# Interleaving the projections and the attention ranges of two head groups, token tile by token tile

## The chip, the cores and the metric

The kernel runs on the 8 cores of one Trainium2 chip. Every core runs the same program on one prompt sequence of 2048 tokens and four of the 32 sample tokens, so each core handles 2052 token columns. No data goes from core to core. The time is that of the device, in microseconds, of the slowest core.

## The reference

One step of a hybrid decoder layer:

```
x += 0.5 * SwiGLU(RMSNorm(x))                         # half-step FFN 1
z  = RMSNorm(x) @ w_in                                # one input projection
A: 3 groups x 4 heads x 128, (window, dilation) = (128,1), (512,4), (2048,16)
   query t reads keys t, t-d, ..., t-window; the three outputs of a head slot are
   merged with weights proportional to their softmax denominators
B: HGRN2 recurrence, 4 heads, state 128x128
C: 4-head cross attention into 256 memory tokens
x += (sum of gate_i * branch_i @ w_i) @ w_out
x += 0.5 * SwiGLU(RMSNorm(x)); final RMSNorm
```

D_MODEL is 1024 and D_FF 2816. Besides y, the kernel returns the last keys and values of each group, the memory keys and values, the recurrent states and the shifted caches of the sample tokens.

## The kernel before, in words

The program has three parts: FFN 1 (to about 495 us of the profiled span), the mixer stage with the branches A, B and C (about 495 to 1030 us), and the merge with FFN 2. The change lies in branch A of the middle stage.

**Order of the work.** The kernel is written as a list of operations with read and write dependencies (class `Prog`). A planner orders them for each engine when the program is built. An operation's priority is the TensorE time written ahead of it in its branch; `merge` stretches the three branches ("att" over 0 to 1, "hg" over 0.03 to 0.97, "mem" over 0 to 0.95) over the same stretch of time. On each engine the planner takes the ready operation of lowest priority number. A buffer is given out only to one of the first n waiting requests of its pool, where n is the number of free buffers. On the chip each engine then runs its list in order and waits on semaphores.

**Pools.** `ps`: 8 PSUM banks, which the whole kernel shares. `wp`: 6 buffers for weights (`wload`, issued by GpSimd, with a lead of 45000 ns on the priority). `s4`: 11 buffers of 128x2048 bf16, for q, k, v and P16. `s1`: 18 buffers of 128x512 bf16. `fw`: 8 buffers of 128x512 f32.

**Branch A, head slot s** (`att_head`). Group 2 (dilation 16) comes first: `att_group` loads its weights, projects q and k (`qk_proj`, five token tiles `QT` of 416, 416, 416, 400 and 404 columns, 8 matmuls each), then v (`v_proj`, four ranges of 512 tokens, 32 matmuls with 128 columns each, and the sample columns). Four score banks give P16. Then group 1 (dilation 4) is projected whole, then group 0 (dilation 1) is projected whole, and then `att_range` runs for R = 0, 1, 2, 3 in a row. A range of 512 tokens is 11 to 16 score matmuls into three or four banks, one exp per bank on ScalarE, one mask multiplication per bank on VectorE, four to five additions on VectorE for the denominators, 31 to 32 matmuls into the bank `num`, one matmul with ones into `den`, Ln and Exp for the reciprocal on ScalarE, and one multiplication on VectorE. `att_sample` ends the head.

**Dependencies.** Each of q, k, v has a single dependency record for its 2048 columns: a copy of one tile into it waits for all matmuls written earlier that read any part of it.

**Pacing.** `pace`, called at the end of each range, marks a point after which SyncE may issue one of the cache copies (`spread`, DRAM to DRAM); the copies are assigned to the nearest mark. Most matmuls are recorded at line 703 (`mm`), ScalarE functions at 707 and 709, copies at 714 and 716, `tensor_tensor` at 722, weight loads at 739. Line 1134 clears 128 columns once per head, in range 0.

Of the kernel before, what the change touches and what calls it, by code (L numbers as in the profile page):

```python
# [595 lines left out]
QT = [(0, 416), (416, 416), (832, 416), (1248, 400), (1648, 404)]  # L596
# [3 lines left out]
def build_nc():  # L600
# [3 lines left out]
    def din(name, shape):  # L604
        return nc.dram_tensor(name, list(shape), F32, kind="ExternalInput").ap()
# [13 lines left out]
    w_qkv = din("w_qkv", [12, 128, 3072])  # L619
# [38 lines left out]
    def xrb(byte0, nbytes):  # L658
        return xr[:, byte0 // 4:(byte0 + nbytes) // 4].bitcast(BF16)
    s4 = P.pool("s4", [xrb(i * 4096, 4096) for i in range(8)] + [xrb(HA * 4 + i * 4096, 4096) for i in range(3)])  # L660
# [38 lines left out]
    def hdeps(c, t0, n):  # L699
        return [dh[i][c] for i in range(6) if TOFF[i] < t0 + n and t0 < TOFF[i] + TW[i]]  # L700

    def mm(o, l, r, start, stop, rd, wr):
        P.op(PE, lambda e: e.matmul(o(), lhsT=l(), rhs=r(), start=start, stop=stop, skip_group_check=True), reads=rd, writes=wr)  # L703
# [7 lines left out]
    def evac(o, i, rd, wr, engs=(ACT, DVE)):  # L711
        alts = {}
        if ACT in engs:
            alts[ACT] = lambda e: e.copy(out=o(), in_=i())  # L714
        if DVE in engs:
            alts[DVE] = lambda e: e.tensor_copy(out=o(), in_=i())  # L716
        if POOL in engs:
            alts[POOL] = lambda e: e.tensor_copy(out=o(), in_=i())
        P.flex(alts, reads=rd, writes=wr)
# [17 lines left out]
    def wload(src, ncols, lead=45000.0, after=()):  # L737
        b = wp.new()
        P.dma(POOL, lambda e: e.dma_start(out=b.t[:, 0:ncols], in_=src), reads=list(after), writes=[b.d], lane="w", lead=lead)  # L739
        return b  # L740
# [300 lines left out]
    def proj(wv, t0, n, wd, fm=True):  # L1041
        pb = ps.new()
        for c in range(8):
            mm(lambda: pb.t[:, 0:n], lambda c=c: wv(c), lambda c=c: ht[:, c, t0:t0 + n], c == 0, c == 7, [wd] + hdeps(c, t0, n), [pb.d])
        return pb

    def tok_bank(wv, blocks, wd):
        pb = ps.new()
        for q, (t0, st) in enumerate(blocks):
            for c in range(8):  # L1050
                mm(lambda q=q: pb.t[:, q * 128:(q + 1) * 128], lambda c=c, t0=t0, st=st: ht[:, c, t0:t0 + 127 * st + 1:st], lambda c=c: wv(c),
                   q == 0 and c == 0, q == 3 and c == 7, [wd] + hdeps(c, t0, 127 * st + 1), [pb.d])
        return pb

    def qk_proj(s, g, kind, wv, wd, zs, dst):
        win, dil = WIN[g]
        L = T // dil
        for t0, n in QT:
            pb = proj(wv, t0, n, wd)
            m = min(n, T - t0)  # L1060
            ov = lambda t0=t0, m=m: dst.t.rearrange("p (r l) -> p r l", r=dil)[:, :, t0 // dil:(t0 + m) // dil]
            lo = max(t0, T - win)
            if kind == 1 and lo < t0 + m:
                sb = fw.new()
                evac(lambda pb=pb, sb=sb, n=n: sb.t[:, 0:n], lambda pb=pb, n=n: pb.t[:, 0:n], [pb.d], [sb.d])
                evac(ov, lambda sb=sb, m=m: sb.t[:, 0:m].rearrange("p (i r) -> p r i", r=dil), [sb.d], [dst.d], engs=(ACT, DVE))
                dd = Dep()
                P.dma(SP, lambda e, sb=sb, lo=lo, t0=t0, m=m: e.dma_start(out=o_k[g][s, :, lo - (T - win):t0 + m - (T - win)], in_=sb.t[:, lo - t0:m]),
                      reads=[sb.d], writes=[dd], lane="out")
                outs.append(dd)  # L1070
                src = sb
            else:
                evac(ov, lambda pb=pb, m=m: pb.t[:, 0:m].rearrange("p (i r) -> p r i", r=dil), [pb.d], [dst.d])
                src = pb
            if n > m:
                z0 = (kind * 3 + g) * 4
                evac(lambda: zsv(zs)[:, z0:z0 + 4], lambda src=src, m=m, n=n: src.t[:, m:n], [src.d], [zs.d], engs=(ACT, DVE))
# [6 lines left out]
    def zsv(zs):  # L1084
        return zs.t

    def v_proj(s, g, wv, wd, zs, dst):
        win, dil = WIN[g]
        for R in range(4):
            if g == 2:  # L1090
                blocks = [(4 * R + j, 16) for j in range(4)]
            elif g == 1:
                blocks = [(512 * R + j, 4) for j in range(4)]
            else:
                blocks = [(512 * R + 128 * j, 1) for j in range(4)]
            pb = tok_bank(wv, blocks, wd)
            ov = lambda R=R: dst.t[:, R * 512:(R + 1) * 512]
            if g == 2 or R == 3:
                sb = fw.new()
                evac(lambda sb=sb: sb.t[:, :], lambda pb=pb: pb.t[:, :], [pb.d], [sb.d])  # L1100
                evac(ov, lambda sb=sb: sb.t[:, :], [sb.d], [dst.d], engs=(ACT, DVE))
                dd = Dep()
                if g == 0:
                    P.dma(SP, lambda e, sb=sb: e.dma_start(out=o_v[0][s, 0], in_=sb.t[:, 384:512]), reads=[sb.d], writes=[dd], lane="out")
                else:
                    b0 = 4 * R if g == 2 else 0
                    P.dma(SP, lambda e, sb=sb, b0=b0: e.dma_start(out=o_v[g][s, b0:b0 + 4].rearrange("b p n -> p b n"),
                                                                  in_=sb.t[:, :].rearrange("p (b n) -> p b n", b=4)), reads=[sb.d], writes=[dd], lane="out")
                outs.append(dd)
            else:  # L1110
                evac(ov, lambda pb=pb: pb.t[:, :], [pb.d], [dst.d])
        pb = proj(wv, T, NS, wd)
        z0 = (6 + g) * 4
        evac(lambda: zsv(zs)[:, z0:z0 + 4], lambda: pb.t[:, 0:4], [pb.d], [zs.d])

    def att_group(s, g, zs):
        wb = wload(w_qkv[s * 3 + g], 3072)
        wv = lambda k: (lambda c: wb.t[:, (k * 8 + c) * 128:(k * 8 + c + 1) * 128])
        q, k, v = s4.new(), s4.new(), s4.new()
        qk_proj(s, g, 0, wv(0), wb.d, zs, q)  # L1120
        qk_proj(s, g, 1, wv(1), wb.d, zs, k)
        v_proj(s, g, wv(2), wb.d, zs, v)
        return q, k, v

    def score_bank(pairs, q, k, mask, dm, dst, ddst):
        pb = ps.new()
        lo = min(j for j, _, _ in pairs) * 128
        for x, (j, k0, q0) in enumerate(pairs):
            mm(lambda j=j: pb.t[:, j * 128:(j + 1) * 128], lambda k0=k0: k.t[:, k0:k0 + 128], lambda q0=q0: q.t[:, q0:q0 + 128],
               x == 0, True, [k.d, q.d], [pb.d])  # L1130
        actf(lambda: dst()[:, lo:512], lambda: pb.t[:, lo:512], AF.Exp, [pb.d], [ddst], scale=SCALE)
        tt(lambda: dst()[:, lo:512], lambda: dst()[:, lo:512], lambda: mask[:, lo:512], ALU.mult, [ddst, dm], [ddst], engs=(DVE,))
        if lo:
            P.op(POOL, lambda e: e.memset(dst()[:, 0:lo], 0.0), writes=[ddst])

    def att_head(s):
        zs = ZS(s)
        q16, k16, v16 = att_group(s, 2, zs)
        P16 = s4.new(4)
        for R in range(4):  # L1140
            score_bank([(j, (4 * R + j) * 128, (4 * R + j) * 128) for j in range(4)], q16, k16, m_own, dmo,
                       lambda R=R: P16.t[:, R * 512:(R + 1) * 512], P16.ds[R])
        q4, k4, v4 = att_group(s, 1, zs)
        q1, k1, v1 = att_group(s, 0, zs)
        for R in range(4):
            att_range(s, R, q4, k4, v4, q1, k1, v1, v16, P16)
        att_sample(s, zs)

    def att_range(s, R, q4, k4, v4, q1, k1, v1, v16, P16):
# [336 lines left out]
    for s in range(4):  # L1486
        att_head(s)
# [210 lines left out]
```

How the kernel before makes its waits and increments, by code:

```python
                def body(e):  # L566
                    for o in order[name]:
                        for s, k in o["waits"]:
                            e.wait_ge(sems[s], semval[s][k])
                        inst = o["fn"](e)
                        if o["sig"]:
                            inst.then_inc(sems[o["stream"]], 16 if o["dma"] else 1)
```

## Time and profile before

| | us |
|---|---|
| median of 3 runs (1807.59, 1811.49, 2007.27) | 1811.49 |
| the profiled execution | 1809.89 |
| its span on the slowest core (core 4) | 1808.3 |
| its spans on the 8 cores | 1794.4 to 1808.3 |
| TensorE busy on core 4 | 1741.8 |

The profiled execution lies between 1807.59 and 1811.49, and its time is 1.6 us more than the span of its slowest core.

### The profile page before, as it was taken

To read this page: it belongs to the slowest core of one execution; us is meant where nothing else is said; L and a number is where in the kernel's file an instruction comes from. 1 tells how busy PE (TensorE), PEld (TensorE's weight loads), DVE (VectorE), ACT (ScalarE), POOL (GpSimd) and SP (SyncE) were. 2 spreads that over 40 slices of the span, in tenths; PEclk is the share of its full clock that TensorE was granted. 3 is DMA by queue.
4 is the path that set the end of the run, shared out by engine and by line. 5 is a ranking of instruction groups with operands and counts; after the bars stand their busy time and mean duration, and the time that the engine had idled before them with its cause. 6 is when DMAs were issued, how large, how long until landed. Compare 5 with 4: busy or idle time off the path is not lost.

```text
span 1808.3 us, 36700 instructions; the slowest of 8 cores (1794.4 to 1808.3 us)
## 1 busy us (share of the span) xinstructions
PE 1741.8 (96%) x13730; PEld 1186.6 (66%) x13809; DVE 805.4 (45%) x1686; ACT 682.5 (38%) x1370; POOL 117.2 (6%) x224
## 2 busy tenths in 40 slices
PE   5999999999999899899899899999999999999997
PEld 2666666666666666666666766666666666666665
DVE  4223643222454645744754744674582222522225
ACT  4323231211256666676576622342242111321212
POOL 0000200000100000000000000000000000000000
PEclk9999999999999999999999999999999999999999
DMA  7845655457864452371661684584556564574632
GB/s 164 176 82 89 134 112 117 77 104 141 161 138 83 91 123 61 86 148 25 119 133 37 145 193 100 99 213 97 113 102 126 105 139 95 135 168 95 138 61 94
DMA packets 61803, 208.77 MB, mean 115 GB/s; under 512 B 7744, under 2 KB 29760, under 8 KB 59712
## 3 DMA queue, kind: packets, MB, share of 16 engines
q0 software_dynamic: 27648, 113.26, 38.3%
q1 hardware_dynamic: 33840, 93.14, 17.2%
q8 instruction: 114, 1.87, 0.4%
q14 instruction: 57, 0.47, 0.1%
q10 hardware_dynamic: 144, 0.03, 0.0%
HBM read 289.42 MB, written 74.22 MB: 201 GB/s over the span
## 4 chain that ended last, share of the span: by engine, by line
PE 89%; DVE 4%; issue 3%; DMA 2%; ACT 2%; DVEq 0%; SPq 0%; another core or an unknown queue 0%; ACTq 0%; POOL 0%; POOLq 0%
PE ps L703 89%; DMA xr<-x_in 2%; DVE xr L722 1%; DVE ht L726 1%; ACT xr L707 1%; DMA xd_scratch<-xr 1%; DVE fw L722 0%; ACT fw L707 0%; DVE xr L726 0%; PE ps L1294 0%; ACT fw L731 0%; DVE ar L722 0%; ACT fw L709 0%; DVE fw L1277 0%; DVE S L1327 0%
## 5 line engine op out<-in xcount | busy, mean ns | idle before, releaser
L703 PE MATMUL ps<-ht,wr 128*128 128x342 bf16 (+6 forms) x6862 | 1123.7, 313 | 7.9 <-DVE ht L726 4.1
L703 PEld LDWEIGHTS ps<-ht,wr 128*128 128x128 bf16 x6912 | 660.6, 98 | 349.3 <-issue 14.4
L707 ACT ACTIVATE fw<-ps 128x342 f32<-128x342 f32 (+3 forms) x472 | 223.1, 475 | 637.8 <-PE ps L703 629.3
L703 PE MATMUL ps<-ar,wr 128*128 128x342 bf16 (+2 forms) x2652 | 406.5, 308 | 0.7 <-DVE fw L722 0.7
L703 PEld LDWEIGHTS ps<-ar,wr 128*128 128x128 bf16 x2652 | 258.7, 98 | 126.6 <-issue 1.0
L722 DVE TENSOR_TENSOR ar<-ps,fw 128x342 bf16<-128x342 f32 (+3 forms) x288 | 150.7, 528 | 424.9 <-PE ps L703 416.4
L703 PE MATMUL ps<-wr,ht 128*128 128x128 bf16 x2080 | 198.0, 221 | 2.2 <-issue 0.6
L731 ACT ACTIVATE fw<-xr 128x342 f32<-128x342 f32 (+4 forms) x170 | 81.1, 489 | 298.6 <-DVE xr L726 244.1
L703 PEld LDWEIGHTS ps<-wr,ht 128*128 128x128 bf16 x2080 | 155.8, 114 | 25.8 <-issue 3.6
L722 DVE TENSOR_TENSOR fw<-fw 128x342 f32<-128x342 f32 (+5 forms) x231 | 123.8, 543 | 63.6 <-ACT fw L731 55.2
L703 PE MATMUL ps<-xr 128*128 128x128 bf16 (+3 forms) x1219 | 131.7, 226 | 12.6 <-DVE xr L722 5.3
L722 DVE TENSOR_TENSOR fw<-ps,fw 128x342 f32<-128x342 f32 (+2 forms) x144 | 73.6, 514 | 104.4 <-PE ps L703 102.6
L726 DVE SCALAR_TENSOR_TENSOR xr<-ps,xr 128x342 f32<-128x342 f32 (+2 forms) x96 | 48.8, 514 | 138.2 <-PE ps L703 138.2
L703 PEld LDWEIGHTS ps<-xr 128*128 128x128 bf16 x1236 | 85.6, 101 | 33.2 <-issue 19.0
L739 POOL DMA_DIRECT2D wr<-w_gu x88 | 46.8, 532 | 590.0 <-PE ps L703 558.2
L707 ACT ACTIVATE xr<-ps 128x512 bf16<-128x512 f32 (+5 forms) x148 | 73.0, 530 | 22.1 <-PE ps L703 20.8
L726 DVE SCALAR_TENSOR_TENSOR ht<-xr,vec,fw 128x342 bf16<-128x342 f32 (+2 forms) x144 | 71.3, 572 | 9.8 <-ACT fw L707 8.7
L714 ACT CAST xr<-ps 128x416 bf16<-128x416 f32 (+2 forms) x88 | 47.0, 534 | 38.6 <-PE ps L703 36.4
L716 DVE CAST xr<-ps 128x512 bf16<-128x512 f32 (+2 forms) x56 | 35.0, 625 | 55.2 <-PE ps L703 50.4
L1327 DVE SCALAR_TENSOR_TENSOR S<-S,ebt,ps 128x128 f32<-128x128 f32 x124 | 42.8, 345 | 32.6 <-ACT xr L714 19.6
L722 DVE TENSOR_TENSOR xr<-xr 128x512 bf16<-128x512 bf16 (+1 forms) x84 | 51.4, 630 | 11.0 <-ACT xr L707 9.2
L707 ACT ACTIVATE fw<-fw 128x512 f32<-128x512 f32 (+5 forms) x93 | 52.8, 576 | 4.8
(117 smaller groups left out, 768.4 us busy)
## 6 DMA issues: line engine op xcount, KB each, us to landing
wr<-w_gu POOLq DMA_DIRECT2D x88, 512.0 KB, 6.1
wr<-w_dn POOLq DMA_DIRECT2D x30, 704.0 KB, 7.7
wr<-w_mg POOLq DMA_DIRECT2D x16, 768.0 KB, 7.5
wr<-w_qkv POOLq DMA_DIRECT2D x12, 768.0 KB, 9.3
wr<-w_mg POOLq DMA_DIRECT2D x16, 384.0 KB, 7.1
xd_scratch<-xr SPq DMA_DIRECT2D x32, 171.0 KB, 4.9
xr<-xd_scratch SPq DMA_DIRECT2D x4, 1368.0 KB, 10.6
y_out<-xr SPq DMA_DIRECT2D x16, 342.0 KB, 4.6
```

The lines of the kernel that those rows point to most:

```text
L703: P.op(PE, lambda e: e.matmul(o(), lhsT=l(), rhs=r(), start=start, stop=stop, skip_group_check=True), reads=rd, writes=wr)
L707: P.op(ACT, lambda e: e.activation(out=o(), in_=i(), func=func, scale=scale), reads=rd, writes=wr, lead=lead)
L714: alts[ACT] = lambda e: e.copy(out=o(), in_=i())
L716: alts[DVE] = lambda e: e.tensor_copy(out=o(), in_=i())
L722: f = lambda e: e.tensor_tensor(out=o(), in0=a(), in1=b(), op=op)
L726: P.op(DVE, lambda e: e.scalar_tensor_tensor(out=o(), in0=a(), scalar=s, in1=b(), op0=op0, op1=op1), reads=rd, writes=wr)
L731: alts[ACT] = lambda e: e.activation(out=o(), in_=i(), func=AF.Square)
L739: P.dma(POOL, lambda e: e.dma_start(out=b.t[:, 0:ncols], in_=src), reads=list(after), writes=[b.d], lane="w", lead=lead)
L1327: P.op(DVE, lambda e, q=q, cc=cc, su=su: e.scalar_tensor_tensor(out=S(), in0=S(), scalar=ebv()[:, cc:cc + 1], in1=su.t[:, q * 128:(q + 1) ...
```

## The change

`att_head` no longer projects groups 1 and 0 whole ahead of the four ranges. It asks for the weights of both groups and for all six q, k, v buffers at once. Then it goes through the five token tiles: for each tile it projects q and k of both groups; from the second tile on, it also projects v of both groups for range t-1 and runs that range. Tile t reaches at least 512 t tokens, so range t-1 has what it reads. `qk_proj` and `v_proj` take the tiles or ranges as an argument; the sample columns of v come with range 3. Every matmul, copy, exp, addition and DMA stays; the order in which they are written changes, and with it their priorities, the time for which a buffer is held, and the marks of the cache copies.

```diff
-        q4, k4, v4 = att_group(s, 1, zs)
-        q1, k1, v1 = att_group(s, 0, zs)
-        for R in range(4):
-            att_range(s, R, q4, k4, v4, q1, k1, v1, v16, P16)
+        near = []
+        for g in (1, 0):
+            wb = wload(w_qkv[s * 3 + g], 3072)
+            near.append((g, wb, qkv_view(wb), [s4.new(), s4.new(), s4.new()]))
+        (q4, k4, v4), (q1, k1, v1) = near[0][3], near[1][3]
+        for t in range(5):
+            for g, wb, wv, bufs in near:
+                for k in range(2):
+                    qk_proj(s, g, k, wv(k), wb.d, zs, bufs[k], QT[t:t + 1])
+            if t:
+                for g, wb, wv, bufs in near:
+                    v_proj(s, g, wv(2), wb.d, zs, bufs[2], (t - 1,))
+                att_range(s, t - 1, q4, k4, v4, q1, k1, v1, v16, P16)
         att_sample(s, zs)
...
-    def qk_proj(s, g, kind, wv, wd, zs, dst):
+    def qk_proj(s, g, kind, wv, wd, zs, dst, tiles=QT):
...
-        for t0, n in QT:
+        for t0, n in tiles:
...
-    def v_proj(s, g, wv, wd, zs, dst):
+    def v_proj(s, g, wv, wd, zs, dst, ranges=(0, 1, 2, 3)):
...
-        for R in range(4):
+        for R in ranges:
...
+        if 3 not in ranges:
+            return
         pb = proj(wv, T, NS, wd)
```

## Rows read from the trace of the kernel before

**Rows 1.** The page's head and its busy times (us, share, count).

```profile
span 1808.3 us, 36700 instructions; the slowest of 8 cores (1794.4 to 1808.3 us)
...
PE 1741.8 (96%) x13730; PEld 1186.6 (66%) x13809; DVE 805.4 (45%) x1686; ACT 682.5 (38%) x1370; POOL 117.2 (6%) x224
```

**Rows 2.** Stretches of 20 us, core 4: length, busy time and count by engine, clock, DMA.

```profile
580.00:600.00 20.00, 19.73 (x230) 14.74 (x234) 9.43 (x20) 13.18 (x29) 0.00 (x0) 1.00 0.02 5
600.00:620.00 20.00, 15.71 (x220) 12.82 (x220) 18.87 (x36) 17.55 (x35) 0.81 (x2) 1.00 0.62 149
620.00:640.00 20.00, 18.13 (x138) 10.13 (x140) 11.88 (x36) 8.74 (x24) 1.06 (x2) 0.74 0.56 121
...
740.00:760.00 20.00, 16.32 (x236) 13.23 (x239) 19.90 (x51) 15.61 (x37) 0.74 (x2) 1.00 0.54 145
760.00:780.00 20.00, 18.77 (x143) 11.25 (x142) 9.46 (x23) 10.85 (x24) 0.53 (x1) 1.00 0.85 159
...
860.00:880.00 20.00, 17.67 (x284) 15.71 (x287) 15.65 (x36) 14.62 (x34) 1.26 (x3) 1.00 0.39 73
880.00:900.00 20.00, 14.25 (x182) 11.27 (x183) 14.88 (x33) 9.86 (x22) 1.06 (x2) 0.93 0.89 163
...
1000.00:1020.00 20.00, 17.10 (x250) 14.48 (x250) 13.78 (x33) 13.92 (x35) 1.26 (x3) 1.00 0.69 121
1020.00:1040.00 20.00, 17.91 (x178) 12.72 (x180) 15.69 (x38) 14.35 (x23) 0.53 (x1) 1.00 0.73 187
```

**Rows 3.** The one memset of each head's range 0: durations in ns, first and last start.

```profile
L1134 POOL MEMSET xr<- x4: 205/205/207, 602.6 to 1012.7; 128x128 bf16 x4
```

**Rows 4.** Stretches of 5 us within the first burst, same columns as rows 2.

```profile
610.00:615.00 5.00, 3.12 (x33) 1.92 (x31) 5.00 (x10) 4.64 (x10) 0.00 (x0) 1.00 0.83 211
...
625.00:630.00 5.00, 5.00 (x46) 2.59 (x44) 2.94 (x13) 2.14 (x9) 0.53 (x1) 0.50 1.20 211
```

**Rows 5.** What TensorE waited for, 495 to 1032 us: total, times, longest.

```profile
PE ps L703 <- DVE xr L722: 12.3, 19, 1.8
PE ps L703 <- issue: 5.2, 4, 4.1
```

**Rows 6.** The same on core 3, 860 to 910 us, and three spans.

```profile
PE ps L703 <- issue: 5.5, 1, 5.5
```

```profile
core 3: 1807.7 us, clock 0.990
core 4: 1808.3 us, clock 0.992
...
core 6: 1794.4 us, clock 0.995
```

**Rows 7.** Groups by form, 495 to 1032 us: busy, mean ns of one | idle before.

```profile
L707 ACT ACTIVATE xr<-ps 128x512 bf16<-128x512 f32 x120 | 67.9, 602 | 9.7 <-PE ps L703 8.8 <-remote 0.6
L722 DVE TENSOR_TENSOR xr<-xr 128x512 bf16<-128x512 bf16 x76 | 50.1, 679 | 10.3 <-ACT xr L707 9.2 <-POOL xr L1134 0.4
...
L722 DVE TENSOR_TENSOR xr<-xr,m_own 128x512 bf16<-128x512 bf16 x48 | 19.5, 419 | 1.6 <-ACT xr L707 1.3
```

**Rows 8.** The chain in order of time, one piece: start, us, what.

```profile
1028.90 149.78 PE ps L703 x1044
```

**Rows 9.** GpSimd's loads in order of time, third head: start, duration, what, idle before.

```profile
762.18 0.53 POOL L739 DMA_DIRECT2D wr<-w_qkv  x1 [8.21 <-PE ps L703]
780.67 0.53 POOL L739 DMA_DIRECT2D wr<-w_qkv  x1 [17.96 <-PE ps L703]
784.32 0.53 POOL L739 DMA_DIRECT2D wr<-w_hg  x1 [3.12 <-PE ps L703]
...
836.00 0.53 POOL L739 DMA_DIRECT2D wr<-w_mq  x1 [35.27 <-PE ps L703]
870.38 0.53 POOL L739 DMA_DIRECT2D wr<-cs_att  x1 [33.85 <-PE ps L703]
...
873.70 0.53 POOL L739 DMA_DIRECT2D wr<-w_qkv  x1 [0.42 <-PE ps L703]
```

**Rows 10.** All loads of that line, 480 to 1040 us: from issue to landing.

```profile
DMA to landing us min/median/max: 4.7/8.7/21.2
```

More of the change, by code:

```diff
@@ L1114, in v_proj, with qkv_view @@
         evac(lambda: zsv(zs)[:, z0:z0 + 4], lambda: pb.t[:, 0:4], [pb.d], [zs.d])
+    def qkv_view(wb):
+        return lambda k: (lambda c: wb.t[:, (k * 8 + c) * 128:(k * 8 + c + 1) * 128])
     def att_group(s, g, zs):
         wb = wload(w_qkv[s * 3 + g], 3072)
-        wv = lambda k: (lambda c: wb.t[:, (k * 8 + c) * 128:(k * 8 + c + 1) * 128])
+        wv = qkv_view(wb)
         q, k, v = s4.new(), s4.new(), s4.new()
```

## The prediction

> **What bounds the kernel now.** I read the page's head first: TensorE is busy 1741.8 of 1808.3 us [rows 1], so no change of order can win more than the 66.5 us in which it is idle, and what a lower clock costs. Then I cut the mixer stage into stretches of 20 us. A quiet stretch shows TensorE at 19.73 of 20 us, and VectorE at 9.43. Eight stretches in four pairs look otherwise: there TensorE is idle 4.29 + 1.87, 3.68 + 1.23, 2.33 + 5.75 and 2.90 + 2.09 us, 24.1 us in all, and VectorE rises to 18.87 and 19.90 of 20 [rows 2]. The memset that marks range 0 of each head comes at 602.6 us the first time and at 1012.7 us the last [rows 3], so the pairs are the four places where a head's four ranges stand in a row. Within the first, VectorE is busy 5.00 of 5 us while TensorE has 3.12; fifteen microseconds later TensorE is full again, but at a granted clock of 0.50, the lower of its two levels (1.2 GHz in place of 2.4) [rows 4]. The waits name the same cause: 12.3 us in 19 waits for a VectorE addition or multiplication [rows 5]. The stage is thus bound by TensorE, except for some 20 us per head in which VectorE binds.
>
> One hole is of another kind: a wait of 4.1 us on core 4 that the profile puts down to nothing [rows 5], just before 898 us; core 3 has it too, with 5.5 us. These two cores have spans of 1808.3 and 1807.7 us; core 6, with 1794.4, is the fastest [rows 6]. The metric is the slowest core, so this wait counts.
>
> **The change part by part.** All sums are made against the profiled execution's 1809.89 us (span and 1.6 us around it), which lies within 0.1% of the median, 1811.49.
>
> *The holes at the ranges.* From the 24.1 us I take off what a quiet stretch also loses, eight times 0.27, and the 4.1 us that belong to no range: 24.1 - 2.2 - 4.1 = 17.8 us, or 1.1 us for each of 16 ranges. Now each range gets the next tile's projections behind it as cover. What must be covered: after the last score four exps of 0.602 us and a mask of 0.419 us until `num` may start, 2.8 us; then about four additions of 0.42 to 0.68 us until `den`, some 2.7 us more: 5.5 us [rows 7]. What covers it: the merge stage shows 1044 matmuls of 342 columns in 149.78 us, 0.1435 us each [rows 8]; by that, 32 matmuls of 416 columns take 5.6 us, and 64 of 128 columns for the next v at least 3.4 us, 9 us in all, beside what the two other branches offer. VectorE's own load of a range is four masks, four additions and a product, some 5 us by the same rows. Four of these in a row on top of the other branches' 9.4 us per 20 us fill it; one in about 20 us leaves it at 15 of 20. So the cover is enough on paper. But the eight PSUM banks bound it: four scores, `num` and `den` want six while the projections want the rest. The bounds of what stays are 0 (a quiet stretch) and 1.1 us per range (as now). I take 0.35, nearer to the quiet stretch because cover exceeds chain: 16 x 0.35 = 5.6 stay, 12.2 us go.
>
> *The clock.* The stretch from 620 to 640 us has a mean clock of 0.74: 0.26 x 20 = 5.2 us of full-speed work are lost right behind the longest run of holes [rows 2]. With holes of a third of a microsecond I expect no such fall: 5.2 us go (bounds 0 and 5.2). The fall behind the unexplained wait at 898 us stays.
>
> *The weights.* Before, the group-1 weights are read only until that group is projected; now both groups' buffers are held until v of range 3. In the third head the two loads were issued at 762.18 and 780.67 us; `w_mq` at 836.00 follows only when a buffer falls free, and `cs_att` at 870.38 and the next head's `w_qkv` at 873.70 when the others do [rows 9]. With one buffer fewer in between, `w_mq` moves to about 870 and stands ahead of the next head's weights. Landing takes 8.7 us by the median, 21.2 at most [rows 10]. Before, the burst of four ranges hid that load; now only one range does. Queued behind this wait on GpSimd are all later loads; who waits is the next head's group 2, while HGRN2 and memory go on. I price it at half a median landing, 4.4 us, at this one place, where the heads of two branches end together (`w_hg` at 784.32 was already in). At the two earlier head ends the next head's weights are asked for first and `w_hg` is the one delayed, with a whole range before it is needed: nothing, and 8.7 us each if that cover is gone. Bounds: 0 and 3 x 8.7 = 26 us.
>
> *The rest.* As many `s4` buffers live at the end of a head as before, eight. The first tiles wait for the group-2 q and k to be freed by the P16 scores, as before. The output DMAs of k and v keep their count on SyncE's queue and leave 10 to 60 us earlier for groups 1 and 0, with nothing waiting for them. The marks of the cache copies now lie evenly apart instead of four in a bunch; DMA share in the bursts goes down (0.89 at 880 to 900 us [rows 2]), which can only bring weights in sooner. In the last head the tail becomes one range instead of four; gate matmuls of the merge stand behind it, and cover it unless their weights are late by the mechanism above (0 to 3 us, I take 0). Waits on other engines' copies: each tile's copy into q or k now waits for the score matmuls of the range two back, which lie ahead of it on TensorE anyway: 0, and see the second rival.
>
> Sum: 12.2 + 5.2 - 4.4 = 13.0 us, 1809.9 - 13.0 = **1797 us**. With the best ends (17.8 + 5.2, no weight wait, and the 4.1 us gone) 1783; with 1.1 us per range kept, clock kept and one full landing added, 1819.
>
> **The rivals.**
>
> *Banks, not VectorE, make the holes.* A range opens six of the eight banks, and the planner keeps banks for earlier requests. Then the holes follow the ranges to their new places: 17.8 us stay, the clock perhaps recovers in part. For it: holes also occur in the pair at 1000 to 1040 us, where VectorE is only 13.78 and 15.69 of 20 [rows 2]. Against it: the waits name VectorE's additions, 12.3 us [rows 5], and VectorE at 5.00 of 5 [rows 4]. Time: 1809.9 + 4.4 - 0 to 5.2 = 1809 to 1814. The Trainium skill ("Perfetto Trace Analysis", Optimization Strategy) says that gaps which repeat on an engine that should be saturated can mean that SBUF or PSUM buffers do not suffice for the next tile; by that rule the time would be that of this rival, 1809 to 1814 in place of 1797. The same section says that regimes bound by different engines may gain from being interleaved, which is the forecast; the rows speak more for the second rule than for the first.
>
> *False dependencies (slower).* One record covers a whole q, k or v. The copy of v for range R+1 has to wait for `num` of range R, its bank stays taken, and the scores of R+1 stand behind the copies of their tile. Where TensorE has less other work than the 2.8 us until `num` may start, each range costs up to 2.8 us at its place between the mask and `num`: at full price 16 x 2.8 = 45 us, less the 17.8 that go, 1809.9 + 27 = 1837; at half price 1809.9 + 22.4 - 17.8 = 1815. It decides as soon as the planner puts less than 2.8 us of projections between scores and `num`. Against it: 5.6 us of the next tile do not depend on the range. 1815 to 1837.
>
> *Weights (slower).* The next head's load is issued only after v of range 3 at all three head ends: 3 x 8.7 = 26 us against the gain of 17.4, 1819.
>
> *It does not do what it says.* The planner reorders by readiness; if it still runs projections ahead of the ranges as far as banks allow, ranges bunch up again: 1806 to 1811.
>
> *More than forecast.* Matmuls that count as busy in the bursts may be slowed too; then over 36 us could go, below 1774.
>
> **How the numbers follow.** Forecast (1783 to 1806) 0.56; banks 0.20; false dependencies 0.11; weights 0.06; not what it says 0.04; more than forecast 0.03. The likeliest gives the time, 1797. From 1783 to 1814 lie the forecast, the banks and the not-what-it-says cases, 0.80. About 2%, 36 us, is what a measurement of this kernel can tell from no change: over 1846 would need false dependencies at more than full price or two mechanisms together, 0.04 with the upper part of both slower rivals; under 1774 has 0.03; between them 0.93.
>
> **What would show it.** Right: the eight stretches with ranges gone, TensorE over 19 of 20 us from 520 to 1000, VectorE nowhere above 16 of 20; 12.3 us of waits for VectorE down to some 5; no half clock in the 630s; the memsets earlier within their head. The weight step: `w_mq` and the fourth head's `w_qkv` issued within a few microseconds of each other, and a TensorE hole there of some 4 us. Wrong: sixteen even holes of about 1 us (banks), waits of TensorE for copies at lines 714 and 716 or for masks (false dependencies), or a bunch of three loads at each head's end with TensorE idle behind it (weights). A new wait that the profile cannot name, on some cores alone, would also spoil it, since the slowest core is what counts.

## The result and the profile after

The changed kernel takes 1787.56 us (1786.51, 1787.72, 1787.39; the kernel before 1807.59, 1811.49 and 1811.52 beside it): 0.9873 of the time before, 95% interval 0.9851 to 0.9895, or 24 us less, where 13 were forecast. One execution of each kernel, 1981.28 and 2007.27 us, was disturbed on one half of the chip and is left out. The profiled execution took 1786.51 us.

The page's head and its first busy time, as [rows 1]:

```profile
span 1784.9 us, 36776 instructions; the slowest of 8 cores (1777.4 to 1784.9 us)
...
PE 1741.0 (98%) x13809; PEld 1183.8 (66%) x13809; DVE 803.8 (45%) x1679; ACT 680.7 (38%) x1377; POOL 116.7 (7%) x224
```

The two busy times can't be set against each other: the trace of core 4 before lacks 79 of the 13809 matmul records. Core 3 before has them all; its span of 1807.7 us has TensorE busy for 1748.7 us. So the same matmuls now take 7.7 us less, and the other 15 of the 23 us between the two spans are idle time. Stretches of 20 us on the slowest core, 5, with the columns of [rows 2]:

```profile
600.00:620.00 20.00, 18.31 (x264) 14.32 (x262) 15.14 (x42) 14.30 (x33) 1.58 (x3) 1.00 0.78 156
620.00:640.00 20.00, 20.00 (x109) 10.68 (x108) 6.01 (x13) 10.75 (x26) 0.53 (x1) 0.91 0.84 165
...
740.00:760.00 20.00, 20.00 (x204) 13.35 (x202) 12.51 (x38) 12.72 (x33) 1.63 (x4) 1.00 0.95 200
...
880.00:900.00 20.00, 19.20 (x164) 11.90 (x163) 10.01 (x24) 12.82 (x26) 0.53 (x1) 1.00 1.03 175
```

The bursts are gone: VectorE peaks at 15.14 of 20 us instead of 19.90, and of all stretches from 500 to 1020 us the one with the least TensorE is that at 600 us, with 18.31. The memset of range 0, as [rows 3], comes 50 us earlier in the first head:

```profile
L1139 POOL MEMSET xr<- x4: 204/204/204, 552.8 to 946.7; 128x128 bf16 x4
```

What TensorE waited for from 495 to 1020 us, as [rows 5]:

```profile
PE ps L703 <- DVE xr L722: 6.6, 14, 0.8
PE ps L703 <- DVE xr L716: 1.9, 5, 0.6
PE ps L703 <- issue: 1.2, 1, 1.2
PE ps L703 <- DMA wr<-cs_att: 0.2, 1, 0.2
```

The waits for VectorE's additions are halved (12.3 to 6.6 us, longest 1.8 to 0.8), and the waits that the profile puts down to nothing ("issue"; nameless waits from here on) are down from 5.2 us to 1.2.

**The ledger.** For the balance I take core 3 of the kernel before (span 1807.7 us): core 4's trace has fewer matmul records (996 against 1023 from 640 to 740 us), and a missing one looks like idle time. The mixer stage of core 3 before, in stretches that hold the stage's start and the four bursts, columns as in [rows 2], with the sum over all stretches from 495 to 1040 us:

```profile
495.00:515.00 20.00, 16.19 (x94) 8.82 (x93) 12.13 (x28) 9.54 (x20) 3.42 (x1) 0.91 0.65 136
...
600.00:640.00 40.00, 34.34 (x369) 22.90 (x366) 30.70 (x71) 26.78 (x60) 1.83 (x4) 0.91 0.81 136
...
740.00:790.00 50.00, 44.77 (x490) 31.70 (x488) 36.14 (x86) 33.36 (x72) 2.11 (x4) 1.00 0.78 148
...
860.00:920.00 60.00, 51.09 (x595) 37.59 (x593) 41.36 (x95) 36.17 (x76) 2.84 (x6) 0.94 0.78 143
...
1000.00:1040.00 40.00, 36.82 (x424) 28.55 (x422) 29.65 (x70) 28.22 (x58) 1.79 (x4) 0.96 0.70 157
sum 545.00, PE 517.21 PEld 365.29 DVE 311.69 ACT 357.56 POOL 21.38; mean PE 57.47 PEld 40.59 DVE 34.63 ACT 39.73 POOL 2.38
```

The same stretches on core 5 after:

```profile
495.00:515.00 20.00, 20.00 (x156) 12.78 (x155) 16.09 (x36) 12.03 (x23) 4.26 (x1) 1.00 0.49 112
...
600.00:640.00 40.00, 38.31 (x371) 25.00 (x370) 21.15 (x55) 25.05 (x59) 2.11 (x4) 0.96 0.81 161
...
740.00:790.00 50.00, 50.00 (x530) 35.79 (x528) 28.33 (x75) 35.13 (x76) 3.36 (x7) 1.00 0.75 160
...
860.00:920.00 60.00, 59.20 (x633) 42.08 (x630) 32.62 (x82) 41.32 (x90) 3.70 (x7) 1.00 0.75 152
...
1000.00:1040.00 40.00, 39.62 (x334) 27.69 (x332) 22.90 (x52) 19.25 (x34) 3.24 (x6) 1.00 1.01 222
sum 545.00, PE 534.06 PEld 376.86 DVE 322.14 ACT 362.88 POOL 24.33; mean PE 59.34 PEld 41.87 DVE 35.79 ACT 40.32 POOL 2.70
```

Idle is 545 less the sum: 27.8 us before, 10.9 after. What the clock took is one less the granted clock, times the length: 1.8 + 3.6 + 3.6 + 1.6 = 10.6 us before, 1.6 after. Split by place, with the nameless waits of that core (1.1 and 5.5 us before, 1.2 after) taken out of the bursts:

| us | before | after | gain | forecast |
|---|---|---|---|---|
| start of the stage, 495 to 515, idle and clock | 5.6 | 0 | 5.6 | 0 |
| bursts 16.4 and the rest 1.0, now 1.7 and 8.1 | 17.4 | 9.8 | 7.6 | 12.2 |
| nameless waits | 6.6 | 1.2 | 5.4 | 0 |
| clock behind bursts and nameless waits | 8.8 | 1.6 | 7.2 | 5.2 |
| weights at the third head's end | 0 | (in the bursts) | 0 | -4.4 |
| sum | 38.4 | 12.6 | 25.8 | 13.0 |

The spans differ by 22.8; the clock is given in hundredths and ends are modelled, so some 3 us of the sum are not sharp. Core 3 is among the worst of its kernel: averaged over the eight cores, idle time and clock took 32.1 us before and 12.0 after, a gain of 20. Eleven of the 25.8 us came from two kinds of wait for which the forecast had no gain. Both have to do with the cache copies. SyncE's queue around the stage's start, kernel before, core 4 (start, duration, instruction, times):

```profile
486.90 1.22 SPq L768 DMA_DIRECT2D o_s1k<-cw1k  x2
489.82 9.77 SPq L862 DMA_DIRECT2D xd_scratch<-xr  x2
```

and after, core 5:

```profile
486.93 0.52 SPq L768 DMA_DIRECT2D o_s1k<-cw1k  x1
489.85 9.75 SPq L862 DMA_DIRECT2D xd_scratch<-xr  x2
```

Before, two copies of 1022 KB stood ahead of the last spills of `xr` (its contents written to DRAM). The spills of 171 KB from 486 to 500 us, first before (core 4), then after (core 5), with the median us to landing:

```profile
xd_scratch<-xr SPq DMA_DIRECT2D x2, 171.0 KB, 13.7
xd_scratch<-xr SPq DMA_DIRECT2D x2, 171.0 KB, 8.5
```

The first memory norm writes into the memory that the spill reads, so ScalarE waited for the spill, and TensorE for the norm (1.8 to 3.8 us on all eight cores). Core 3 before:

```profile
ACT xr L1391 <- DMA xd_scratch<-xr: 5.6, 1, 5.6
PE ps L703 <- ACT xr L1391: 3.8, 1, 3.8
```

`pace` sits at the end of each range. With the ranges spread, the marks are spread. Before, the copies of this stage left mostly in pairs, and once as four (from 610 to 627 us on core 4); after, they leave one by one but for three pairs (559, 692 and 1012 us on core 5).

### The profile page after: what moved, and what is told of

It is laid out like the page before. It is cut to its first block, busy times and chain, and to the rows that moved or that the text cites. A ratio compares the mean times of both kernels' runs of the same rounds, so it can differ in the third digit from the quotient of the medians.

```text
span 1784.9 us, 36776 instructions; the slowest of 8 cores (1777.4 to 1784.9 us)
## 1 busy us (share of the span) xinstructions
PE 1741.0 (98%) x13809; PEld 1183.8 (66%) x13809; DVE 803.8 (45%) x1679; ACT 680.7 (38%) x1377; POOL 116.7 (7%) x224
## 3 DMA queue, kind: packets, MB, share of 16 engines
q1 hardware_dynamic: 33840, 93.14, 17.4%
q8 instruction: 114, 1.87, 0.4%
## 4 chain that ended last, share of the span: by engine, by line
PE 89%; DVE 4%; issue 2%; DMA 2%; ACT 2%; DVEq 0%; SPq 0%; ACTq 0%; POOLq 0%
PE ps L703 88%; DVE xr L722 2%; DMA xr<-x_in 2%; DVE ht L726 1%; DMA wr<-cs_att 1%; DVE fw L722 0%; ACT fw L707 0%; ACT xr L707 0%; DVE fw L1291 0%; ACT fw L709 0%; ACT fw L1289 0%; DVE xr L726 0%; ACT fw L731 0%; PE ps L1308 0%; DVE xr L716 0%
## 5 line engine op out<-in xcount | busy, mean ns | idle before, releaser
L703 PE MATMUL ps<-ht,wr 128*128 128x342 bf16 (+7 forms) x6912 | 1142.8, 313 | 6.2 <-DVE ht L726 4.1
L703 PE MATMUL ps<-wr,ht 128*128 128x128 bf16 (+1 forms) x2080 | 196.0, 221 | 0.0
L703 PEld LDWEIGHTS ps<-wr,ht 128*128 128x128 bf16 (+1 forms) x2080 | 154.5, 114 | 25.8 <-issue 2.9
L707 ACT ACTIVATE xr<-ps 128x512 bf16<-128x512 f32 (+3 forms) x148 | 72.6, 532 | 10.1 <-PE ps L703 9.8
L716 DVE CAST xr<-ps 128x512 bf16<-128x512 f32 (+2 forms) x51 | 32.1, 632 | 44.4 <-PE ps L703 44.1
```

The costliest lines, as they stand in the source:

```text
L707: P.op(ACT, lambda e: e.activation(out=o(), in_=i(), func=func, scale=scale), reads=rd, writes=wr, lead=lead)
```

## The experiments

Ratios are to the kernel before, measured on the same chip beside each experiment.

**Is it the early request for weights and buffers?** The old order, with both groups' loads and six buffers asked for at once (`near` as in the change):

```diff
-        q4, k4, v4 = att_group(s, 1, zs)
-        q1, k1, v1 = att_group(s, 0, zs)
+        for g, wb, wv, bufs in near:
+            for k in range(2):
+                qk_proj(s, g, k, wv(k), wb.d, zs, bufs[k])
+            v_proj(s, g, wv(2), wb.d, zs, bufs[2])
```

> The order of the kernel before, but the weights of groups 1 and 0 and all six buffers are asked for at once, as in the change. Main theory (the four ranges in a row overload VectorE): the bursts stay, TensorE idle 20 us or more in them, and the weights are only held longer: 1808 to 1822 us, ratio 0.998 to 1.006. Rival (the early second load gives TensorE work at the start of the stage and at the head ends, and that is the gain): 1785 to 1797 us, ratio 0.985 to 0.992.

1.0006 (0.9994 to 1.0017). The waits are those of before (12.1 us for additions, 4.7 nameless). The requests are worth nothing either way.

**Is it the order of the projections, or of the ranges?** The change, with the ranges in a row at the end:

```diff
-                att_range(s, t - 1, q4, k4, v4, q1, k1, v1, v16, P16)
+        for R in range(4):
+            att_range(s, R, q4, k4, v4, q1, k1, v1, v16, P16)
```

> The projections of groups 1 and 0 interleaved tile by tile as in the change, but the four ranges of a head left in a row behind them. Main theory: the four bursts come back with VectorE at 18 of 20 us or more and TensorE idle about 5 us per burst: 1804 to 1816 us, ratio 0.996 to 1.002. Rival (interleaving the projections, with its other order of copies and loads, is what helps): 1785 to 1795 us.

1.0014 (0.9999 to 1.0029), waits for additions 12.4 us in 19. All of the gain hangs on where the ranges stand, and with them the marks of the copies, which this run leaves at the heads' ends too.

**Half the change.** Group 1 projected whole by `att_group`; only group 0 tile by tile:

```diff
-            for g, wb, wv, bufs in near:
-                for k in range(2):
-                    qk_proj(s, g, k, wv(k), wb.d, zs, bufs[k], QT[t:t + 1])
+            for k, buf in enumerate((q1, k1)):
+                qk_proj(s, 0, k, wv(k), wb.d, zs, buf, QT[t:t + 1])
```

> Group 1 projected whole, only group 0 interleaved tile by tile with the ranges; the group-1 weights are free early, as before. A range then has half the projections behind it as cover, about 4.5 us against a chain of 5.5 us. Main theory: between the two kernels, 1789 to 1801 us, ratio 0.988 to 0.994, with VectorE at 16 to 18 of 20 us in the stretches with ranges. If cover of its own branch does not matter because the two other branches fill in: as the change, 1785 to 1789. If holding the weights longer cost the change something: below it, 1780 to 1785.

0.9943 (0.9926 to 0.9961): less than half of the gain. Waits for additions 9.0 us, and the copies still leave mostly in pairs, with the wait at the start (2.9 us) and a nameless one of 2.7.

**What do VectorE's additions cost, in either order?** All denominator additions but the first of each range are left out, so the denominators lack terms; once in the old order and once in the change:

```diff
-        tt(nsn, nsn, v16n, ALU.add, [ns.d] + P16.ds, [ns.d], engs=(DVE,))
...
-            tt(n4, n4, lambda: nat4(n2.t), ALU.add, [ns.d, n2.d], [ns.d], engs=(DVE,))
```

> The kernel before with all but one of VectorE's additions for the denominators left out (the sums over group 2 and group 1 are missing from the denominators); all matmuls, exps, masks, banks and their order stay as written. Main theory (VectorE binds in the bursts): the load of a burst falls by some 10 of 20 us of VectorE, and most of the holes and the half clock go: 1785 to 1799 us, ratio 0.985 to 0.993. Rival (the banks are short): the holes stay, 1804 to 1812 us, ratio 0.996 to 1.000.

> The change with all but one of VectorE's additions for the denominators left out, as in e4_before_no_adds (denominators incomplete). If VectorE's bursts were what the change removed, leaving the additions out has little left to give: 2 to 7 us, since TensorE still waits 6.6 us in 14 waits for them: ratio 0.983 to 0.987. If the additions cost as much here as in the kernel before (0.9924, some 14 us): 0.977 to 0.981.

Old order: 0.9924 (0.9902 to 0.9947), 14 us; waits for additions 12.3 to 1.6 us, while the start's wait (4.3) and 4.6 us of nameless waits stay. Change: 0.9832 (0.9806 to 0.9858) against 0.9873, some 7 us. So the step on the holes named the right engine, and half of its price is still there after the change.

**Are banks short?** The change with seven PSUM banks:

```diff
-    ps = P.pool("ps", [nc.alloc_psum_tensor(f"ps{i}", [128, 512], F32) for i in range(8)], psum=True)
+    ps = P.pool("ps", [nc.alloc_psum_tensor(f"ps{i}", [128, 512], F32) for i in range(7)], psum=True)
```

> The change with seven PSUM banks instead of eight. If banks bind the new order (the rival of the prediction), one bank less costs each of 16 ranges some 0.5 to 1 us: ratio 0.992 to 0.998, TensorE's holes growing at the ranges. If they do not: 0.986 to 0.990.

0.9903 (0.9880 to 0.9927); one bank less costs some 5 us, with an interval that overlaps that of the change. The eighth bank is used, but there is no sign of a shortage that sets sixteen holes; and with eight banks nearly all of what is left of the waits for additions goes when the planner alone is put right (below).

**What do the copies' marks do alone?** In the old order, the marks moved to four points spread over the projections of groups 1 and 0:

```diff
+            if g < 2 and kind == 1 and t0 == QT[2][0]:
+                pace(dst.d)
...
+        if g < 2:
+            pace(dst.d)
...
-        pace(dbrs(0, s, R * 512))
```

and in the change, marks at the heads' ends alone, which lets the copies leave in fours there:

```diff
-        pace(dbrs(0, s, R * 512))
+        if R == 3:
+            pace(dbrs(0, s, R * 512))
```

> The order of the kernel before; only the marks for the cache copies are moved from the four ranges at a head's end to four points spread over the projections of groups 1 and 0, so that one copy instead of two stands ahead of the last spill at 490 us and the copies leave one by one. Theory that the copies are a part of the gain: the wait of TensorE at 507 to 510 us and the nameless wait behind the third head's end go (3 to 4 us and 4 to 5 us on the slowest cores, with the low clock behind them), the four bursts stay: ratio 0.990 to 0.996, some 1794 to 1804 us where the kernel before has 1811.5. Rival (only the VectorE bursts count): 0.998 to 1.002.

> The change with the marks of the cache copies at range 3 alone, so that the copies leave in bunches at each head's end and two stand ahead of the last spill, as before; everything else as in the change. Theory that the copies are a part: the wait at the start of the stage comes back, and one at a head's end may: ratio 0.990 to 0.995 against 0.9873 for the change. Rival (only the bursts count): 0.986 to 0.989.

Spread marks in the old order: 0.9952 (0.9935 to 0.9969), 8.7 us, though the bursts stay (9.7 us of waits for additions). Copies in fours in the change: 1.0063 (1.0044 to 1.0082), which is 34 us above the change and slower than before. Its bad stretch, core 1:

```profile
800.00:820.00 20.00, 11.08 (x76) 6.37 (x75) 4.56 (x10) 8.82 (x16) 0.53 (x1) 0.74 0.80 176
```

What ScalarE waited for there, 495 to 1040 us:

```profile
ACT fw L714 <- DMA o_k<-fw: 8.5, 1, 8.5
ACT fw L709 <- DMA o_k<-fw: 8.2, 1, 8.2
```

and the issues from 740 to 830 us (what, times, KB, median us to landing):

```profile
o_s2k<-cw2k SPq DMA_DIRECT2D x1, 1022.0 KB, 34.0
...
o_k<-fw SPq DMA_DIRECT2D x3, 208.0 KB, 32.7
```

The outputs of k stand behind four copies on SyncE's queue and land after 32.7 us. Until then they hold their `fw` buffers, of which there are eight; ScalarE waits for one, and TensorE for ScalarE. By their size these are k tiles of group 2 (416 columns x 128 x 4 bytes), which begins the next head: marks at the heads' ends put four copies right ahead of them. The weight loads that come in a bunch at the same place are not what is named.

**Is it the size of the bunch?** The change with marks at ranges 1 and 3 only, copies in pairs:

```diff
-        pace(dbrs(0, s, R * 512))
+        if R % 2:
+            pace(dbrs(0, s, R * 512))
```

> The changed kernel, with the pace marks kept only at ranges 1 and 3 of each head: eight marks for the cache copies in place of sixteen, so they leave two at a time. Single copies gave 0.9873, bunches of four at the head ends 1.0063. If the time goes with the size of a bunch, two at a time lie between: 0.990 to 0.998, the first pair at about 488 us brings back the wait for the last spill (2 to 4 us, clock about 0.91 in 500 to 520 us), and landings behind a pair take some 15 us. If only a bunch of four on top of the weight loads at a head's end hurts, pairs cost no more than the start: 0.987 to 0.990, no TensorE stretch of 20 us under 18 after 520 us.

0.9935 (0.9919 to 0.9951): singles 0.9873, pairs 0.9935, fours 1.0063. Most of the pairs' price is at the start. Core 1, the stretch and ScalarE's wait:

```profile
495.00:515.00 20.00, 15.44 (x79) 7.84 (x78) 11.19 (x25) 9.42 (x18) 3.18 (x1) 0.85 0.69 152
```

```profile
ACT xr L1406 <- DMA xd_scratch<-xr: 6.4, 1, 6.4
```

That is 4.6 us idle and 3.0 of clock, where the change has none; over the eight cores 5.2 and 2.8 on average.

**Then is the start's wait alone worth 5 us before?** Only the second copy of the pair at 486.90 us is moved, behind the first head's first score bank:

```diff
-            bulk_one(i, s_, d_)
+            bulk_one(late[0] if k == 11 else i, s_, d_)
```

> The kernel before with a single cache copy moved: of the two that leave at 486.90 and 487.5 us, ahead of the last two spills of xr, the second is tied to the first score of group 2 in the first head, some 40 us later; the four-copy bunches stay. If the second copy is what holds up the spill, TensorE's wait at the start of the mixer stage (1.8 to 3.8 us, all eight cores) goes and the clock in 500 to 520 us rises from 0.91 to 1.00: 3.2 us of idle time and 1.8 us of clock, about 5 us, ratio 0.996 to 0.998; the rest of the 8.7 us that spread marks gave on this order then belongs to the later bunches and their wait before 898 us, which stays here. If the spill is late for another reason, the wait stays and the ratio is 0.999 to 1.001.

0.9997 (0.9986 to 1.0007). The wait did go, on every core, and nothing was won. Core 3, the start and the first burst:

```profile
495.00:515.00 20.00, 20.00 (x160) 12.94 (x158) 15.46 (x35) 12.19 (x24) 3.62 (x1) 1.00 0.38 108
...
600.00:640.00 40.00, 35.61 (x292) 22.30 (x293) 26.74 (x64) 21.77 (x50) 1.05 (x2) 0.74 0.71 134
```

In the first burst the clock now takes 0.26 x 40 = 10.4 us instead of 3.6. Averaged over the eight cores it takes 8.3 here and 6.1 with the spread marks, the two runs of the old order without a wait at the start; in the kernel before (2.0) and the three other runs of the old range order, which keep that wait, 0.7 to 3.0. So where the hole at the start is filled, the clock falls deeper at the next, 100 us later, and takes the gain back. The kernel before shows the same among its cores: on cores 1 and 5 the clock did not fall at the start, and it took 3.6 us in the first burst; of the other six, where it did fall, four lost nothing there. That the one causes the other is argued from these rows, not shown. In the change there is no burst to pay it back at, and the 5.6 us stay won; pairs in the changed order lose them again. Of the two expectations, one had the wait right and the time wrong, the other the reverse.

**What are the waits that are left?** Two of the additions in each range are strided: one operand is read with 128 elements between neighbours. Here is the change, with strided bfloat16 additions planned at the 1.04 us that they take, not at 0.34:

```diff
+        elif p.kind == "tensor_tensor" and p.bf and p.dims == 3:
+            p.occ = 75 + 1.88 * p.n
```

> The changed kernel, with one formula of the planner corrected: a strided bfloat16 addition of 128x512 is planned at 1.04 us, as the trace shows, in place of 0.34 us. Two of them stand in each range's chain to den, so the planner puts the den matmul some 1.4 us too early. If what is left of TensorE's waits for VectorE (6.6 us in 14, nearly all before den) comes from that, they fall under 3 us and the ratio to the kernel before is 0.983 to 0.986. If they are set by VectorE's load or by the banks, they stay at 5 us or more and the ratio stays at 0.986 to 0.989.

0.9836 (0.9818 to 0.9853), 1782.22 us, the shortest time of a kernel that leaves nothing out. In the change, the additions of the first range (ns, least, median, most) were

```profile
L722 DVE TENSOR_TENSOR xr<-xr x3: 413/1033/1050, 553.2 to 555.1; 128x512 bf16<-128x512 bf16 x3
```

and the `den` matmuls, grouped by form, stood 6.4 us idle:

```profile
L703 PE MATMUL ps<-xr,ones_b 128*128 128x512 bf16 x48 | 17.8, 378 | 6.4 <-DVE xr L722 6.1 <-DVE xr L716 0.3
```

With the corrected cost:

```profile
L706 PE MATMUL ps<-xr,ones_b 128*128 128x512 bf16 x48 | 18.7, 389 | 0.0
```

TensorE's waits for additions fall from 6.6 us to 0.2. So what stayed of the holes was mostly not VectorE's load: the planner put `den` too early.

**Do the shared dependency records cost anything?** The change, with a record for each tile of q and k and each range of v:

```diff
-            near.append((g, wb, qkv_view(wb), [s4.new(), s4.new(), s4.new()]))
+            near.append((g, wb, qkv_view(wb), [s4.new(5), s4.new(5), s4.new(4)]))
```

> The changed kernel with dependency records for each token tile of q and k and for each range of v, in groups 1 and 0, in place of one for the whole buffer: a copy of a later tile no longer waits for the matmuls of an earlier range. If the false dependencies cost something in the change, TensorE's waits for copies (1.9 us in 5 on VectorE's) go, the scores come earlier, and the ratio is 0.982 to 0.986. If they cost nothing, 0.986 to 0.989, with the waits for den unchanged at 6 to 7 us.

0.9869 (0.9854 to 0.9885): nothing.

## Why the prediction was right, and where it was not

**Holes.** Right in place and engine, too large: 7.6 us in place of 12.2. The 17.8 us to start from were read on core 4, where a missing matmul record looks like a hole; core 3 has 16.4. The bursts lost 14.7 us (16.4 to 1.7), but the quiet stretches, now with a range in them every 33 us, went from 1.0 to 8.1 us idle. I let 0.35 us per range stay; (1.7 + 8.1) / 16 = 0.61 did. I had read VectorE's additions as 0.42 to 0.68 us from a row that puts contiguous and strided ones of one shape together [rows 7]; the two strided ones take 1.03 and 1.05, and the planner, which counts 0.34, sends `den` ahead of them.

**Clock.** Forecast 5.2 us, got 7.2, of which 3.6 lay behind the nameless wait. The single stretch at 0.74 [rows 2] was that of core 4; core 3 lost 3.6 us there, and four of the eight cores nothing. After, the one fall that is left, 0.91 from 620 to 640 us on core 5, stands right behind its nameless wait of 1.2 us (restart at 619.5); the other seven cores show none there.

**The rest, and the hole of 4.1 us.** This is the step that failed. I priced the cache copies' marks at 0 ("which can only bring weights in sooner") and let the nameless wait stay; together with the start's wait, which I had not listed, they gave 11.0 us. I had looked at a copy as a load on the DMA engines, not as an entry in SyncE's queue with spills and outputs behind it. The sentence that the outputs of k and v leave "with nothing waiting for them" held only because the copies came singly: behind four of them, ScalarE waited for the buffers. How the gain divides between copies and order is not a plain sum. Spread marks alone gave 8.7 us, the order with copies in fours lost 11, and both together gave 24. The nearest to the order alone is the run with copies in pairs, as they mostly left before: 0.9935, or 11.8 us, close to the 13 that were forecast for the order. What it gives with the copies at exactly their old times was not tried.

**Weights.** The bunch came as described, GpSimd's loads on core 5 as [rows 9]:

```profile
866.53 0.53 POOL L739 DMA_DIRECT2D wr<-w_mq  x1 [51.21 <-PE ps L703]
871.33 0.53 POOL L739 DMA_DIRECT2D wr<-cs_att  x1 [4.28 <-PE ps L703]
873.59 0.53 POOL L739 DMA_DIRECT2D wr<-w_qkv  x1 [1.73 <-PE ps L703]
```

but TensorE lost 0.80 us there, 0.2 of it for a load. Half a landing was too much: the last range and the other branches covered all of it.

**Rivals.** Banks: the time is not 1809 to 1814, and a bank less costs 5 us; the Trainium skill's rule on repeating gaps ("Perfetto Trace Analysis", Optimization Strategy) pointed away from the cause here, its remark on interleaving towards it. False dependencies: 1.9 us of waits for copies at line 716, and finer records change nothing. Weights at all three ends, and "does not do what it says": neither. The time lies in the range in part by luck. Its low end, 1783, allowed for the nameless wait to go and the weights to cost nothing, which came true; but it also had all 17.8 us of holes gone, where 7.6 went, and the start's 5.6 us, which stood nowhere in the sum, made up for a good part of that. The prediction also took 36 us for the least that can be told from no change; the intervals here are some 2 to 5 us to either side.

## What to carry to other kernels

Before moving a stage, list what else is hung on its position: here a pacing mark at the end of each range decided when 1-MB copies enter a queue that also carries spills and outputs, and that was worth as much as the move itself. Price a DMA by what is queued behind it and by the buffers that these hold, not by its bandwidth. And count a filled hole as a gain only when the stretches behind it have been looked at too: here a later fall of the clock took one back.

## What was not expected of the hardware

**TensorE seems to wait for its own instructions.** The wait that the profile puts to nothing, core 3 before (start, duration, what, idle before it):

```profile
898.36 0.39 PE L703 MATMUL ps<-xr 128*128 128x128 bf16 x1 [5.53 <-issue]
```

In the ten microseconds from 885 to 895 the DMA queues of that core moved (packets, MB, share of 16 engines)

```profile
q1 hardware_dynamic: 32, 1.05, 50.2%
q0 software_dynamic: 8, 0.05, 4.7%
```

so the copies' queue moved one megabyte, the weights' queue next to nothing, and the queue named "instruction" nothing. On core 6, which has no such wait, the same ten microseconds show

```profile
q0 software_dynamic: 212, 1.20, 98.5%
...
q8 instruction: 1, 0.02, 0.7%
```

On core 3 the next instruction packet comes between 895 and 896 us:

```profile
q8 instruction: 1, 0.02, 9.1%
```

TensorE starts some 3 us later. Five kernels, all cores taken, have 47 nameless waits of over 1 us in the mixer stage: 9 before, 1 after, 12 with one copy moved, 6 with spread marks, 19 with copies in fours. In all 47 such a packet starts 2.2 to 3.2 us ahead of the restart, though the page counts only 114 of them in the span, one in 16 us. The Trainium skill ("Runtime: NRT & Kernel Launch", Instruction fetch mechanics) says that the sequencer fetches instructions in 16 KiB blocks by a DMA queue of its own, and that a block boundary is mostly hidden. The block agrees (1.87 MB in 114 packets are 16.4 KB each); "mostly hidden" does not hold behind the copies, where it cost up to 9.2 us. That the copies delay the packet is seen from the queues and from the number of such waits in each kernel; the packet's own way was not seen.

**One core of each pair loses.** Before, the spans of cores 0 and 1, 2 and 3, and so on are 1804.7 and 1795.7, 1798.5 and 1807.7, 1808.3 and 1797.5, 1794.4 and 1803.6 us. Cores 0, 3, 4 and 7 are the ones with a nameless wait of 3.6 to 5.5 us after the third head. Over 44 runs of the kernel before, the two cores of a pair differ by 10.2 us on average, over three of the change by 3.8. About 6 of the 24 us were won on the slower core of each pair alone. The Trainium skill ("HBM Reference", Specifications) says that the two cores of a pair share the bandwidth of one memory; the pairs are seen here, what they share was not tested.

**The clock's debt.** Both kernels of the old order that have no hole at 510 us show a deeper fall at 620 us (8.3 and 6.1 us, against 0.7 to 3.0 in the four that have it), and so do the two cores of the kernel before whose clock did not fall at the start. Whether the one brings the other about, and what in TensorE's work decides the depth, stays open.
